# First layer's MLP: the up product as seven block products, and its down-weight sums moved into the input projection

## The reference

```
xp = xp + rms(mixer(rms(xp, g0)), g1)
xp = xp + rms(square(relu(rms(xp, g2) @ w1)) @ w2, g3)      # w1 1024x4096, w2 4096x1024
```

## Time and profile before

| | us |
|---|---|
| median of three runs | 2173.14 (2172.93 to 2173.84) |
| the profiled execution | 2173.05 |
| its span, first to last instruction | 2171.2 |
| PE busy in the span | 2118.4 (98%) |
| DVE busy | 1026.0 (47%) |
| ACT busy | 818.7 (38%) |

### The profile page before, as it was taken

How to read it: one execution, slowest core, us unless ns; L and a number is a source line. 1 busy time by engine, 2 the same in 40 slices (tenths; PEclk the granted TensorE clock), 3 DMA queues, 4 the chain that set the end, 5 groups by cost and what they waited for, 6 DMA issues and landing times.

```text
span 2171.2 us, 31832 instructions
## 1 busy us (share of the span) xinstructions
PE 2118.4 (98%) x13227; PEld 1912.4 (88%) x13227; DVE 1026.0 (47%) x1503; ACT 818.7 (38%) x1507; POOL 133.8 (6%) x214
## 2 busy tenths in 40 slices
PE   7999999999999999999999999999999999999998
PEld 7999877777789999999888878789999999888886
DVE  5120287566553333333645467663333335444475
ACT  5111397545332223232523245452222224333343
POOL 1000131000110000000000013220000000000011
PEclk9999999999999999999999999999999999999999
DMA  5331301098426666665876553436666566665464
GB/s 172 87 86 36 141 26 34 19 406 329 141 80 225 219 225 217 220 212 217 283 246 228 170 163 98 144 128 229 228 216 226 212 219 235 240 224 169 161 216 137
DMA packets 205963, 394.21 MB, mean 182 GB/s; under 512 B 18749, under 2 KB 100853, under 8 KB 197500
## 3 DMA queue, kind: packets, MB, share of 16 engines
q1 hardware_dynamic: 199628, 387.45, 51.6%
q10 hardware_dynamic: 6192, 4.72, 0.7%
HBM read 273.12 MB, written 119.24 MB: 181 GB/s over the span
## 4 chain that ended last, share of the span: by engine, by line
PE 76%; DVE 2%; ACT 1%; issue 1%; POOL 0%; DMA 0%; POOLq 0%; DVEq 0%; SPq 0%; ACTq 0%
PE ps L1914 34%; PE ps L1953 27%; PE ps L3097 4%; PE ps L1971 3%; PE ps L1413 2%; PE ps L1923 1%; PE ps L3017 1%; PE ps L1434 1%; PE ps L1474 1%; PE ps L2990 1%; PE ps L1455 0%; DMA t_b_raw<-scratch_t_ops 0%; PE ps L3117 0%; PE ps L3030 0%; POOL stats L1529 0%
## 5 line engine op out<-in xcount | busy, mean ns | idle before, releaser
L1953 PE MATMUL ps<-t_b_hi,t_a_hi 128*128 128x512 f32 x896 | 351.7, 393 | 2.1 <-DVE t_y L1823 1.1
L1953 PE MATMUL ps<-t_b_lo,t_a_hi 128*128 128x512 f32 x896 | 348.9, 389 | 0.0
L1953 PE MATMUL ps<-t_b_hi,t_a_lo 128*128 128x512 f32 x896 | 348.9, 389 | 0.0
L1914 PE MATMUL ps<-m_xT_hi,t_w_lo 128*128 128x384 f32 (+1 forms) x1480 | 326.7, 328 | 0.0
L1914 PE MATMUL ps<-m_xT_lo,t_w_hi 128*128 128x384 f32 (+1 forms) x1480 | 326.7, 328 | 0.0
L1914 PE MATMUL ps<-m_xT_hi,t_w_hi 128*128 128x384 f32 (+1 forms) x1480 | 326.7, 328 | 0.0
L1680 DVE TENSOR_TENSOR t_w_lo<-t_raw,t_w_hi 128x1024 fp32r<-128x1024 f32 x64 | 78.3, 1225 | 427.0 <-ACT t_w_hi L1676 427.0
L1744 DVE TENSOR_TENSOR t_a_lo<-t_a_raw,t_a_hi 128x1024 fp32r<-128x1024 f32 x112 | 137.2, 1225 | 300.3 <-ACT t_a_hi L1737 300.3
L1737 ACT ACTIVATE t_a_hi<-t_a_raw 128x1024 fp32r<-128x1024 f32 x112 | 118.8, 1061 | 396.3 <-PE ps L1971 275.8
L1676 ACT ACTIVATE t_w_hi<-t_raw 128x1024 fp32r<-128x1024 f32 x64 | 67.7, 1058 | 504.9 <-PE ps L1914 492.2
L1914 PEld LDWEIGHTS ps<-m_xT_hi,t_w_lo 128*128 128x128 f32 x1480 | 252.9, 188 | 0.0
(11 more groups left out here) (284 smaller groups left out, 3010.2 us busy)
## 6 DMA issues: line engine op xcount, KB each, us to landing
scratch_t_ops<-t_t SPq DMA_DIRECT2D x32, 1280.0 KB, 5.5
scratch_s_ops<-t_s SPq DMA_DIRECT2D x32, 1280.0 KB, 4.5
t_a_raw<-scratch_s_ops SPq DMA_DIRECT2D x80, 512.0 KB, 3.9
t_b_raw<-scratch_t_ops SPq DMA_DIRECT2D x80, 512.0 KB, 4.7
t_raw<-mlp_w SPq DMA_DIRECT2D x64, 512.0 KB, 4.1
t_w_raw<-mlp_w SPq DMA_DIRECT2D x32, 1024.0 KB, 7.7
scratch_a_ops<-t_h SPq DMA_DIRECT2D x32, 512.0 KB, 5.5
t_a_raw<-scratch_a_ops SPq DMA_DIRECT2D x32, 512.0 KB, 3.4
```

The source lines that it names most:

```text
L1914: mm = self.nc.tensor.matmul(out, a[:, k, :], b_[:, k, c], start=(k == 0 and x == 0), stop=(k == KT - 1 and x == 2))
L1953: mm = self.nc.tensor.matmul(self.core.ps[:, self.BANK[idx] + tp, :], a[s][:, kk, tp * P:(tp + 1) * P], w[s][:, kk, :], start=(c == 0 and ...
```

## The change

1. `BlockMlp`, a new class, makes `m0`'s up product. The k dimension is halved (A side and B side) and the tokens of every token tile are halved, so that a pair of hidden tiles by a pair of token halves is a 2x2 block product. It is made with seven products of half the k depth (4 k-steps x 3 passes): A11, A12, A22 and four sums S1 to S4 of weight blocks, against B11, B21, B22 and four sums T1 to T4 of input blocks. Each matmul covers 288 columns (four prompt tiles' halves and half the samples) or 256 columns (the other four tiles' halves), in two PSUM banks with one set of weights: 7 x 4 x 3 x 2 = 168 matmuls for a pair, for 144 before. `m1` keeps its up product.
2. DVE sums weights (`sum_weights`, four of 128x512 per pair), makes lo parts of four groups (three of 128x1024, one of 128x512), adds the products up from PSUM (`hold`, `take_c11`, `take_c22`, `take_c12`, `take_c21`); ACT copies the first product out (`snap`), splits the groups and applies ReLU and square from SBUF.
3. The first pair is made for the first five tiles' columns (`half` 0) while the last token tile is still in its norm, then for the others; sums and splits of x are made in the output projection, per tile for five tiles (`sum_x`, `x_split_hi`, `x_split_lo`) and in two parts for the last four.
4. `combine_t`, its loads of w2 and its stores leave `m0`'s up product. `DownSums` makes the same sums in the input projection, in 64 slices of 128 columns.

The core of the diff for point 4:

```diff
+class DownSums:
+    SLICES = D // 2 // P
+    COUNT = PAIRS * SLICES
+    def load(self, sp, j):
+        if j >= 3:
+            sp.wait_ge(self.ready, j - 2)
...
+        for e in range(2):
...
+            sp.dma_start(self.raw[:, j % 3, e], src).then_inc(self.raw_in[j % 3], 16)
+    def store(self, sp, j):
+        i, x = divmod(j, self.SLICES)
+        sp.wait_ge(self.ready, j + 1)
+        sp.dma_start(self.t_ops[i][:, :, x * P:(x + 1) * P], self.t[:, j % 2]).then_inc(self.stored[j % 2], 16)
+    def move(self, sp, first, last):
+        for j in range(first, last):
+            self.store(sp, j)
+            self.load(sp, j + 3)
+    def combine(self, dve, count):
+        for j in range(self.done, self.done + count):
+            w, t = self.raw[:, j % 3], self.t[:, j % 2]
+            dve.wait_ge(self.raw_in[j % 3], 32 * (j // 3 + 1))
+            if j >= 2:
+                dve.wait_ge(self.stored[j % 2], 16 * (j // 2))
+            nc.vector.tensor_tensor(t[:, 0:2], w[:, :, 0], w[:, :, 1], ALU.add)
+            nc.vector.tensor_tensor(t[:, 2], b11, b22, ALU.add)
+            nc.vector.tensor_tensor(t[:, 3], b12, b22, ALU.subtract)
+            nc.vector.tensor_tensor(t[:, 4], b21, b11, ALU.subtract).then_inc(self.ready, 1)
 (in_project, SP: before the load of chunk n)
+                for j in range(3): down.load(sp, j)          # n == 2
+            if n == 3:   down.move(sp, 0, 3)
+            elif n == 4: down.move(sp, 3, 5)
+            elif n == 5: down.move(sp, 5, 16)
+            elif n == 7: down.move(sp, 16, 28)
+            elif n == 8: down.move(sp, 28, 40)
+        down.move(sp, 40, down.COUNT)
 (in_project, DVE)
+            if i >= 4: down.combine(dve, 1)
+        lo(2)
+        down.combine(dve, 11)
+        lo(3)
         for m in range(Q):
             for n in turns_of(m): take_rows(n)
             if m % 2 == 0: lo(NV + m // 2 + 2)
+            down.combine(dve, 6)
+        down.combine(dve, 12)
         for n in range(NV + 2 + Q // 2, len(chunks)): lo(n)
```

and for point 1, PE's order and waits:

```diff
+    def product(self, pe, p, o, halves=(0, 1)):
+        pe.wait_ge(self.lo_done, self.weights_count(p, o))
+        self.wait_banks(pe, p, o, halves[-1])
+        for k in range(KT // 2):
+            hi, lo = self.left(p, o, k)
+            for x in range(3):
+                for half in halves:
...
+                    mm = self.nc.tensor.matmul(self.part(p, o, half), a, b[:, k, :], ...)
+        mm.then_inc(self.up_ready, 1)
+    def wait_bank(self, pe, idx, tp):
+        if idx == self.M7:
+            pe.wait_ge(self.mixed, self.mixes(last, self.C12 if tp < 2 else self.C21))
 (trunk, PE)
+            m0.product(pe, 0, 0, (0,)); ... m0.product(pe, 0, 4, (0,))
             turn_out(NT - 1)
+            m0.product(pe, 0, 5, (0,)); m0.product(pe, 0, 6, (0,))
+            for o in range(7):
+                pe.wait_ge(m0.x_lo, m0.late_lo_count(1, o))
+                m0.product(pe, 0, o, (1,))
+            for p in range(1, PAIRS):
+                for o in range(7): m0.product(pe, p, o)
 (trunk, DVE, last pair)
+                m0.take_c11(dve, p); m0.hold(dve, p, BlockMlp.U2)
+                m0.split_operands_lo(dve, 0)
+                m0.hold(dve, p, BlockMlp.U3)
+                m0.split_operands_lo(dve, 1)
+                m0.take_c22(dve, p); m0.hold(dve, p, BlockMlp.U4); m0.take_c12(dve, p)
+                m0.split_operands_lo(dve, 2)
+                m0.take_c21(dve, p)
```

More of the change, by code:

```diff
@@ L433, in sync @@
                     load_x(t)
+                for j in range(3):
+                    down.load(sp, j)
+            if n == 3:
+                down.move(sp, 0, 3)
+            elif n == 4:
+                down.move(sp, 3, 5)
+            elif n == 5:
+                down.move(sp, 5, 16)
+            elif n == 7:
+                down.move(sp, 16, 28)
+            elif n == 8:
+                down.move(sp, 28, 40)
             if n >= 2:
@@ L575, in vector @@
                 lo(1)
-        for n in range(2, NV + 2):
-            lo(n)
+            if i >= 4:
+                down.combine(dve, 1)
+        lo(2)
+        down.combine(dve, 11)
+        lo(3)
         for m in range(Q):
@@ L1654, in up_loads @@
     def up_loads(self, sp):
-        for i in range(2):
-            self.load_w2(sp, i)
+        if self.sums_here:
+            for i in range(2):
+                self.load_w2(sp, i)
         for n in range(2 * PAIRS):
@@ L2003 @@
+@dataclass
+class UpMemory:
+    raw: list
+    sums: object
+    group_hi: list
+    group_lo: list
+    first_sums: list
+    first_hi: dict
+    first_lo: dict
+    kept: object
+    first_kept: object
+    x: object
+    early_hi: object
+    early_lo: object
+    early_sum: object
+    late_hi: list
+    late_lo: list
+    late_sum: list
+OUT_TILES = [0, 1, PT] + list(range(2, PT))
 @dataclass
@@ L2270, in _ @@
                     load_x(j + 2)
[L2271 to L2274, removed]
+            sp.wait_ge(out_pre.scaled, NT)
+            for e in range(2):
+                m0.load_weights(sp, 1, e)
+            m0.load_pair(sp, 2)
             m0.up_loads(sp)
@@ L2530, in _ @@
                     split_o(j + 2)
-                take_out_hi(j - 1)
+                take_x(j - 1)
                 act.wait_ge(out_post.squared, j + 1)
                 square_x1(j)
[L2534 to L2543, removed]
+                if j <= BlockMlp.EARLY_TILES:
+                    m0.x_split_hi(act, j - 1, 2)
@@ new lines, in _ @@
+            m0.take_c22(dve, 0, (0,))
+            m0.hold(dve, 0, BlockMlp.U4, (0,))
+            m0.late_sum_lo(dve, BlockMlp.T3)
+            m0.late_sum_lo(dve, BlockMlp.T1)
+            m0.take_c12(dve, 0, (0,))
+            m0.late_split_lo(dve, 1, BlockMlp.B22)
+            m0.take_c21(dve, 0, (0,))
+            m0.late_sum_lo(dve, BlockMlp.T4)
+            m0.weights_lo(dve, 1, 0)
+            m0.take_c11(dve, 0, (1,))
+            m0.hold(dve, 0, BlockMlp.U2, (1,))
+            for s in range(2):
+                dve.wait_ge(x1_stored[s], 16 * len(range(s, NT, 2)))
@@ new lines, in _ @@
+            m0.sum_weights(dve, 1)
+            m0.hold(dve, 0, BlockMlp.U3, (1,))
+            m0.take_c22(dve, 0, (1,))
+            m0.hold(dve, 0, BlockMlp.U4, (1,))
+            m0.weights_lo(dve, 1, 1)
+            m0.take_c12(dve, 0, (1,))
+            m0.take_c21(dve, 0, (1,))
+            m0.weights_lo(dve, 1, 2)
+            m0.weights_lo(dve, 1, 3)
+            m0.combine_s(dve, 0)
+            for p in range(1, PAIRS):
+                if p >= 2:
+                    m0.combine_s(dve, p - 1)
+                    m0.weights_lo(dve, p, 3)
+                m0.take_c11(dve, p)
+                if p + 1 < PAIRS:
+                    m0.sum_weights(dve, p + 1)
+                m0.hold(dve, p, BlockMlp.U2)
+                if p + 1 < PAIRS:
+                    m0.weights_lo(dve, p + 1, 0)
+                else:
@@ L2828, in _ @@
+                m0.hold(dve, p, BlockMlp.U4)
+                m0.take_c12(dve, p)
+                if p + 1 < PAIRS:
+                    m0.weights_lo(dve, p + 1, 2)
+                else:
+                    m0.split_operands_lo(dve, 2)
+                m0.take_c21(dve, p)
+            m0.combine_s(dve, PAIRS - 1)
+            for s in range(3, 40):
                 m0.split_operands_lo(dve, s)
```

598 lines of the change are left out of this document (538 added, 60 removed).

## The result

The changed kernel takes 2182.47 us (median of 5 runs, 2181.17 to 2185.88) against 2173.14 (2172.23 to 2173.94): ratio 1.0046, interval 1.0032 to 1.0061. It is slower by 0.43%, where 2166 and "faster" were forecast. The range held the time, by half a us; the direction was wrong. The profiled execution's span is 2179.3 us, before 2171.2.

A forecast was written before the change was run, and what follows sets the result against it. PE was taken to bound `m0`'s up product and the input projection. From 2173.1 us, 36 less for the up product and seam and 29 more for the slices gave 2166 us, range 2145 to 2183.

The forecast's parts named there:

- What bounds the kernel: `m0`'s up product and input projection: PE bounds both; each us of PE saved in the up product counts.
- Part 1: Steady up product: 1260 couples of 288 and 256 columns at 255.5 ns, 321.9 us, DVE side costed at nothing.
- rival C: Up product: DVE's waits set the pace, at 23 us a pair 22 us lost, 2188 us; chance 0.05.
- Rival D: Up product: couples of 288 and 256 columns cost 231.7 ns, 30 us less, 2136 us; chance 0.03.
- Part 2: First pair of the up product: PE waits 1.0 us for scaling, 0.6 us for late DVE work; over at 667.9.
- Part 3: Seam to the down product: a stop of 5.5 us for DVE's takes, plus 1.7 us of half clock.
- Part 4: 64 slices in the input projection: DVE's store waits stall PE at blocks 2, 4 and 6, 29 us in sum.
- The bound of 43 us: Input projection at 2.7 us a slice: even blocks stall 12, odd ones 2, block 10 waits 5 us.
- The 1.5 us that the prediction puts on it: Slices in the input projection: by the skill's 2.75 us for a 320 KB store, not 2.6, the sum is 1.5 us worse.
- B: Input projection: the queue limits the slices, odd blocks stall too; 46 us lost, 2183 us; chance 0.17.
- my own case: Main forecast: store landings hold the input projection's slices, a round of two in 4.5 us; 2166 us, chance 0.53.
- A: Input projection: the slices are covered, stalls at most 12 us, 2147 us; chance 0.22.

The follow-up runs named there:

- experiment 1: The changed kernel with the 64 slices' sums cut to one, stored in all 64 places: 2138.26 us, ratio 0.9842 to the kernel before.
- experiment 3: The changed kernel with the same 64 slices spread over DVE's list, sixteen ahead of `lo(3)`: 2138.09 us, ratio 0.9844 to the kernel before.
- experiment 5: Spread slices, last pair's operand splits later on DVE, fifth operand's load ahead of the last sums' store on SP: 2130.53 us, ratio 0.9812 to the kernel before.
- experiment 6: The changed kernel with four buffers for the slices' sums instead of two, order unchanged: 2167.91 us, ratio 0.9983 to the kernel before.
- experiment 4: The changed kernel with slices spread over DVE's list and, in the last pair, down operands split later: 2140.96 us, ratio 0.9853 to the kernel before.

## Why the prediction was wrong

**What bounds the kernel**: right. Every us of PE in the up product counted; without the slices (experiment 1) the gain is there.

**Part 1**: right, the term a little large. PE is busy 295.00 of 295.00 us, and 2350 matmuls in them are 1175 couples of 251.1 ns, where 255.5 were taken and 253.3 was the lower bound: under the bound, and about 5 us less over 1260 couples. DVE at 208.84 of 295 us is 71% busy (67% by the forecast of 14.5 in 21.5) and hid as costed; rival C is out. Rival D, 231.7 ns, is out as well. That was the time by the Trainium skill's rule (TensorE: Matmul & The Clock Gate, "Back-to-back issue gap": columns / 2.4 + 2.5 ns, which the page gives for an isolated matmul); couples of 288 and 256 columns do not follow it in this trace either (251.1 ns).

**Part 2**: right in kind. The two waits, 1.25 and 0.67 us, were forecast at 1.0 and 0.6.

**Part 3**: right. PE waits 5.1 us for C12 (5.5 forecast for C12 and C21 together), behind two lo parts of operands; the clock afterwards cost 2.4 for 1.7. Parts 1 to 3 together give 42.4 - 2.4 = 40.0 us less, 36 were forecast.

**Part 4** is the step that failed: "Sum 29 us". It is 46.7 (47.7, since the projection began 1.0 us earlier). The mechanism was right: the order of DVE's list, waits of L643 behind a lo part and a group of slices, three times, ending at 122.3, 160.8 and 200.6 (forecast near 122, 157 and 192). Three terms were mis-sized:

- The half clock: 8.9 us, costed at nothing. The stretch of 0.55 behind a stop of 2.4 us had been read, and was charged for the one stop at the seam and not for stops four times as long. This is half of the miss, and needed no new fact.
- Block 10: a stop of 5.1 us, forecast at none. The last slices came 2.5 us apart and ended at 244.4; only then could `lo(7)` begin, and PE had stood since 241.6. The bound of 43 us had this term in it at 5.
- The three stops: 33.1 us for 29.2. The forecast runs two slices of a round on end, 1.0 us apart. In the last rounds of the three groups the second slice came 2.1, 2.4 and 2.5 us behind the first (118.35 and 120.48 in the group shown), 4 us more in all, because SP needs about 2.0 us for a slice's three DMAs and issues them in order. The landing was hardly mis-sized: 3.6 us, where 2.6 for the store and 0.8 for the loads had been taken.

8.9 + 5.1 + 3.9 = 17.9 against 46.7 - 29 = 17.7. With Part 4 at 47 and the rest as it was, the forecast would have been 2184. That the range held 2182.47 is luck: the 4 us that Parts 1 to 3 gave more than forecast brought the time back under its upper end, 2183.

The price of a store by the Trainium skill (DMA: Bandwidth & Descriptors, "Anatomy of one DMA — SWDGE (gpsimd) path"), an estimated 2.75 us, is one for DMAs that GpSimd issues. These go out on SP's queue, and by the rows they landed after 3.6 us with loads around them and 2.8 without. The 1.5 us that the prediction puts on it would be 0.9, 0.15 us for each of six rounds (three groups of two).

**The rivals.** B's price, 46 us, and its time, 2183, came true, by another way. It said that from about 2.0 us a slice blocks 3, 5 and 7 would stall too. Once a group's stores ran, its slices came 2.15 us apart (114.02 to 120.48), and yet no odd block stalled. That is about the pace of my own case (a round of two in 4.5 us); what B's price was made of is the same three even blocks, the last chunk and the clock. That its number fits is chance. A is out, though what it names can be had: experiment 3 is the case "the slices are covered", at 2138 us and so even below A's 2147.

## What to carry to other kernels

An operation that waits for DMAs costs little on an idle engine if it stands singly between operations that others need (about 5 to 6 us for 64 slices here, most of it where sixteen still stood in a row); six in a row in front of such an operation cost 11 us of PE a time, and more buffers only brought the next limit. Count for every long stop of PE not only its length but the half clock behind it, 1.7 to 2.9 us each here. Where a stall is taken away, ask what is queued behind the instruction that has been hiding under it: the order of three instructions on DVE was worth nothing until one load moved on SP, and then about 5 us.

## What the runs showed of the hardware

Behind every stop of 3.1 us or more that was looked at, the clock fell to the 1.2 GHz level, whatever the stop's length: 0.50 to 0.63 in the first 4 us behind stops of 3.1 and 3.5 (experiment 3), 5.1, 10.7, 10.9 and 11.5 us, and at the seam behind 5.1 us. The loss was 1.7 to 2.9 us each and did not grow with the stop: 1.7 behind 11.5, 2.6 behind 5.1. Shorter stops were mostly free of it: 1.00 behind 1.6 us (experiment 5), 1.9 (the changed kernel at 635.72) and 2.0 (experiment 6). Of two stops of 2.4 to 2.5 us in the kernel before, one was followed by 0.55 and the other by 1.00.

The time of a DMA issue on SP is not a fixed one of the DMA. The two loads of a slice take 1.3 us as a rule; at 82.33 in the changed kernel, with stores of `v` by ACT under way (issued at 76.32), they took 3.47. In the kernel before a weight chunk's four loads took 5.15 us at 81.42, four us behind the same stores, and 2.89 at 107.18. In experiment 4 the first half of an operand, 512 KB, took 0.36 us to issue at 994.39, and the first half of the next 1.32 at 1006.26, right behind the stores of the last sums. Such a figure is to be read from a window without a wait in it: the timeline gives the eight loads of two chunks as one row of 17.04 us from 92.23 on, and 10.6 us of it are SP's wait for DVE.
